# Memory attention on one core: tile 0's weights copied between tile 1's exponentials, tile 1's last transposes and values inside the first output product

## The reference, cut to what matters

```python
def memory_attention(h, mem_n, wq, wkv, wo):
    q = jnp.einsum('bsd,dhe->bshe', h, wq)
    kv = jnp.einsum('bmd,dche->bmche', mem_n, wkv)
    k, v = kv[:, :, 0], kv[:, :, 1]
    logits = jnp.einsum('bshe,bmhe->bhsm', q, k).astype(jnp.float32) * (X_DIM ** -0.5)
    p = jax.nn.softmax(logits, axis=-1)
    o = jnp.einsum('bhsm,bmhe->bshe', p.astype(v.dtype), v)
    return jnp.einsum('bshe,hed->bsd', o, wo)
```

## Time and profile before

| | us |
|---|---|
| median of 3 runs | 3042.37 (3041.61 to 3042.58) |
| the profiled execution's own time | 3040.55 |
| its span | 3038.8 |
| PE busy in the span | 3021.5 |
| ACT busy | 1536.7 |
| DVE busy | 1999.1 |

### The profile page before, as it was taken

The page is one execution under the profiler, slowest core; times in us unless marked ns, Lnnn a source line. Parts: engine busy times, 40 slices in busy tenths (PEclk is TensorE's granted clock), DMA queues, the critical chain, the costliest instruction groups (busy, mean ns, idle before and its releaser), DMA issues.

```text
span 3038.8 us, 43788 instructions
## 1 busy us (share of the span) xinstructions
PE 3021.5 (99%) x15684; PEld 2553.3 (84%) x15684; DVE 1999.1 (66%) x2366; ACT 1536.7 (51%) x2027; POOL 72.6 (2%) x122
## 2 busy tenths in 40 slices
PE   9999999999999999999999999999999999999999
PEld 9888888888888888888888888888888789788887
DVE  6677856555555555777857665655665778888664
ACT  6655546444444444655547455555554555444543
POOL 0000001000000000000000000000000010000000
PEclk9999999999999999999999999999999999999999
DMA  8764554655555555554554666666666555676555
GB/s 333 244 185 162 187 167 158 226 193 190 190 187 192 191 189 189 176 183 160 187 168 157 228 216 206 203 200 205 219 205 209 169 189 189 215 234 221 166 193 173
DMA packets 167930, 596.83 MB, mean 196 GB/s; under 512 B 18846, under 2 KB 26202, under 8 KB 164954
## 3 DMA queue, kind: packets, MB, share of 16 engines
q1 hardware_dynamic: 150432, 545.33, 54.4%
q10 hardware_dynamic: 14888, 36.86, 3.5%
q0 software_dynamic: 2464, 12.67, 1.3%
HBM read 577.99 MB, written 17.07 MB: 196 GB/s over the span
## 4 chain that ended last, share of the span: by engine, by line
PE 90%; DVE 6%; ACT 2%; DVEq 1%; issue 1%; DMA 0%; ACTq 0%; POOL 0%; POOLq 0%; SPq 0%
PE acc L741 24%; PE acc L743 23%; PE acc L742 23%; PE acc L747 3%; PE acc L756 3%; PE acc L759 3%; PE acc L758 3%; DVE lo L2006 2%; PE acc L749 2%; PE tp L831 1%; PE tp L873 1%; PE tp L1040 0%; PE tp L1273 0%; ACT hi L1331 0%; DVE sr L2806 0%
## 5 line engine op out<-in xcount | busy, mean ns | idle before, releaser
L2006 DVE TENSOR_TENSOR lo<-raw,hi 128x1024 fp32r<-128x1024 f32 x1032 | 1245.8, 1215 | 787.0 <-ACT hi L1331 775.8
L1331 ACT ACTIVATE hi<-raw 128x1024 fp32r<-128x1024 f32 x1032 | 1079.6, 1051 | 1133.4 <-PE acc L743 938.0
L741 PE MATMUL acc<-hi,xhl 128*128 128x512 f32 (+2 forms) x2472 | 958.7, 388 | 4.5 <-DVE xhl L2149 2.5
L743 PE MATMUL acc<-hi,xhl 128*128 128x512 f32 (+2 forms) x2472 | 951.2, 385 | 0.0
L742 PE MATMUL acc<-lo,xhl 128*128 128x512 f32 (+2 forms) x2472 | 950.6, 385 | 0.0
L741 PEld LDWEIGHTS acc<-hi,xhl 128*128 128x128 f32 x2472 | 464.3, 188 | 99.9 <-issue 8.1
L743 PEld LDWEIGHTS acc<-hi,xhl 128*128 128x128 f32 x2472 | 464.1, 188 | 92.5
L742 PEld LDWEIGHTS acc<-lo,xhl 128*128 128x128 f32 x2472 | 464.6, 188 | 88.7
L741 PE MATMUL acc<-hi,hTh 128*128 128x512 f32 x640 | 249.1, 389 | 0.0
L743 PE MATMUL acc<-hi,hTl 128*128 128x512 f32 x640 | 249.0, 389 | 0.0
L742 PE MATMUL acc<-lo,hTh 128*128 128x512 f32 x640 | 249.0, 389 | 0.0
(11 more groups left out here) (456 smaller groups left out, 2964.7 us busy)
## 6 DMA issues: line engine op xcount, KB each, us to landing
raw<-in_stream SPq DMA_DIRECT2D x1032, 512.0 KB, 4.2
turn_scratch<-made ACTq DMA_DIRECT2D x8, 1024.0 KB, 6.8
gpost<-in_post_g POOLq DMA_DIRECT2D x6, 1024.0 KB, 8.3
rotc<-turn_scratch ACTq DMA_DIRECT2D x8, 512.0 KB, 6.8
rots<-turn_scratch ACTq DMA_DIRECT2D x8, 512.0 KB, 8.6
u_stack<-u_scratch ACTq DMA_DIRECT2D x24, 128.0 KB, 4.8
h<-in_mem ACTq DMA_DIRECT2D x2, 1024.0 KB, 8.5
xT<-in_x_cols ACTq DMA_DIRECT2D x4, 512.0 KB, 6.7
```

The source lines that it names most:

```text
L741: nc.tensor.matmul(o, ah, high, start=first, stop=False)
L743: last = nc.tensor.matmul(o, al, high, start=False, stop=final)
L1331: nc.scalar.activation(hi[s][:, :, 0:w], raw[s][:, :, 0:w], ACT.Copy).then_inc(hi_done, 1)
L2006: nc.vector.tensor_tensor(lo[s][:, :, 0:w], raw[s][:, :, 0:w], hi[s][:, :, 0:w].bitcast(F32), ALU.subtract).then_inc(split_done, 1)
```

## The change

On ACT, tile 0's two copies (L1698 before) stand ahead of tile 1's second pair of exponentials, and tile 0's high half ahead of tile 1's copies. On PE, the values of tile 0 come straight behind the transposes of tile 0; the transposes (1,1) stand between the two units of `xo0`'s tile 0, and the values of tile 1 between tile 0 and tile 1 of `xo0`. The `stay_warm` matmuls are 4, 2, 2, 2 (10 in all) in place of 4, 3, 1, 1 (9), and the first four no longer wait for the PSUM buffer. DVE, POOL and SP have the same rows in the same order.

```diff
-                        tile_product(pos, LG["xo0"], a_h, a_l, lambda t: pe.wait_ge(x_split, pos.n(2, t + 1)))
+                        tile_product(pos, LG["xo0"], a_h, a_l, between)
...
                 for t in range(NT):
-                    tile_ready(t)
                     for n in range(g.units):
+                        tile_ready(t, n)
...
+                stay_warm(free.parity, xl[:, 8:10, :], 4)
+                weights_across(0, 0)
+                stay_warm(free.parity, xl[:, 8:10, :], 2)
+                weights_across(0, 1)
+                stay_warm(free.parity, xl[:, 8:10, :], 2)
+                head_values(0)
+                weights_across(1, 0)
+                stay_warm(free.parity, xl[:, 8:10, :], 2)
+
+                def second_tile_heads(t, n):
+                    if (t, n) == (0, 1):
+                        weights_across(1, 1)
+                    elif (t, n) == (1, 0):
+                        head_values(1)
+                    if n == 0:
+                        pe.wait_ge(x_split, pos.n(2, t + 1))
+
+                branch_products(pos, 1, "xo", cqh, cql, between=second_tile_heads)
...
+                head_exps(0, 0)
+                head_exps(0, 1)
+                head_exps(1, 0)
+                weights_copy(0, 0)
+                weights_copy(0, 1)
+                head_exps(1, 1)
+                values_high(0)
+                weights_copy(1, 0)
+                weights_copy(1, 1)
+                values_high(1)
```

More of the change, by code:

```diff
@@ L957, in given_rows, with branch_products @@
                 return unit_ready
-            def branch_products(pos, k, tag, a_h, a_l, quad_ready=None):
+            def branch_products(pos, k, tag, a_h, a_l, quad_ready=None, between=None):
                 for n in range(4):
@@ L1141, in _, with weights_across, head_values @@
                 values = acc[LG["xq"].parity]
[L1142 to L1154, removed]
+                def weights_across(i, m):
+                    o = take_turn(pe, pos, LTP[f"xT{i}"]) if m == 0 else tp[LTP[f"xT{i}"] % 2]
+                    pe.wait_ge(x_weights, pos.n(4, 2 * i + m + 1))
+                    for hd in (2 * m, 2 * m + 1):
+                        for b in range(NT):
+                            last = nc.tensor.transpose(o[:, hd, b * P:(b + 1) * P], xe[i][:, hd, b * P:(b + 1) * P],
+                                                       ident[:, :])
+                    last.then_inc((x_across, tp_full)[m], 1)
+                def head_values(i):
                     for m in range(2):
@@ L1161, in _ @@
                     last.then_inc(x_values, 1)
-                branch_products(pos, 1, "xo", cqh, cql)
+                stay_warm(free.parity, xl[:, 8:10, :], 4)
[14 more added lines that the diff above has]
+                branch_products(pos, 1, "xo", cqh, cql, between=second_tile_heads)
                 ready = raw_start(pos, 2, "fpre", LTP, LG["gate0"])
@@ L1680, in _ @@
                 nc.scalar.activation(small[:, 252:253], small[:, 253:254], ACT.Exp)
[L1681 to L1690, removed]
@@ L1691, in _ @@
-                for i in range(NT):
-                    o = tp[LTP[f"xT{i}"] % 2]
[L1693 to L1700, removed]
@@ L1701, in _, with head_exps @@
-                for i in range(NT):
+                def head_exps(i, m):
+                    act.wait_ge(x_max, pos.n(4, 2 * i + m + 1))
+                    o = tp[LTP[f"xL{i}"] % 2]
+                    for hd in (2 * m, 2 * m + 1):
+                        last = nc.scalar.activation(xe[i][:, hd, :], o[:, hd, :], ACT.Exp, scale=rsx[:, i:i + 1],
+                                                    bias=nmx[i][:, hd:hd + 1], accum_out=sm[i][:, hd:hd + 1])
+                    last.then_inc((x_exp, tp_read[LTP[f"xL{i}"] % 2])[m], 1)
@@ new lines, in weights_copy @@
+                def weights_copy(i, m):
+                    o = tp[LTP[f"xT{i}"] % 2]
+                    if m == 0:
+                        act.wait_ge(x_across, pos.n(2, i + 1))
+                    else:
+                        see_turn(act, pos, LTP[f"xT{i}"])
+                    nc.scalar.activation(xz[i][:, 2 * m:2 * m + 2, :], o[:, 2 * m:2 * m + 2, :], ACT.Copy)\
+                      .then_inc(x_copied, 1)
+                    if m == 1:
+                        act.drain().then_inc(tp_read[LTP[f"xT{i}"] % 2], 1)
@@ L1702, in _, with values_high @@
+                def values_high(i):
                     act.wait_ge(x_values, pos.n(2, i + 1))
```

## The result

The changed kernel takes 3045.98 us (median of 22 runs, 3044.53 to 3048.73); the kernel before, measured beside it, 3041.89 us (22 runs, 3039.55 to 3045.95). The ratio is 1.0015, with a 95% interval of 1.0009 to 1.0021: 2.7 to 6.4 us slower, and clear of no change. The forecast was 5.4 us slower, 3047.8, with a range of 3045.4 to 3050.0.

The account below looks back on a forecast made before the run. The prediction took PE to bound the kernel, busy 3021.5 of 3038.8 us. Its terms summed to 2.69 us later in each layer, 5.4 for two, so 3042.4 + 5.4 = 3047.8, range 3045.4 to 3050.0.

Parts of the forecast that it names:

- The chain of 3.37 us: Memory attention: from a tile's first value matmul through ACT and DVE to its product, 3.37 us, 1.62 of it ACT and DVE alone.
- The start of `xo0`: Product start in memory attention: 1.29 us sooner, at 16.72 against 18.01, once tile 0 is split.
- the front of the stage: First fillers and transposes (0,0): these start some 0.5 us sooner, without gain, since transposes (0,1) still wait for DVE.
- The exponentials "at no cost": ACT's exponentials (1,1) behind tile 0's copies: moved to about 13.75 to 14.95, costing nothing on the path, 0.15 us in hand.
- Two fillers more are on the path: PE's work before the products: two extra fillers at 0.23 us each counted as lengthening the path.
- the fourth rival: Whole kernel faster, at most 3041, if DVE finished sooner by some effect on shared PSUM traffic; chance 0.02.
- Tile 0 of `xo0` with the transposes (1,1): Inside the product: tile 0 takes 2.84 us as before, the transposes 0.49 more, so tile 1's values start at 20.05.
- The wait ahead of tile 1: PE before tile 1's product: 1.62 us idle, with nothing left to lie over ACT and DVE.
- The weight unit: ACT's split behind tile 1's high half: moves from 18.78 to 22.6, wanted at 29, cost nothing.
- The dearer joins: Three added fp32r/fp32 changes inside `xo0`: at 0.15 us a join, 3.1 a layer, 3048.6; chance 0.20.
- Later absorption: Behind the stage: part of the delay swallowed later, or the second wait shorter, 3044.3 to 3046; chance 0.12.
- The clock: Idle stretches in the stage: clock falls to half speed for 6 us, 3 us lost, twice, 3053.8; chance 0.06.

## Why the prediction was right, point by point

**The chain of 3.37 us** from a tile's first value matmul to its product. Measured for tile 1: values at 1623.95, product at 1627.31, 3.36 us. ACT's high half starts 1.98 behind the values, DVE's low half 0.63 behind that. This was the term that carried the forecast, and the run that put the values ahead of a unit of the product showed that it is the cause: the chain kept its 3.36 us there, and with a unit over it only 0.2 of the 1.6 us between PE's last slot and the product stayed bare.

**The start of `xo0`**, forecast at 10.94 (1616.72) and measured at 10.93 and 10.92. That it fits within 0.02 is in part luck, since three small errors cancel. "That gives nothing", of the front of the stage, was wrong: before, the transposes (0,1) start 0.19 us behind the end of DVE's product (12.28, then 12.47), not 0.06, so it was the third filler that set them. With one filler less they start 0.05 behind it, at 6.56 in place of 6.69 us, 0.13 sooner. From there to the values it is 0.95 us where 0.88 was forecast, so the values start at 7.51, 7.57 forecast. And from the values to `xo0` it is 3.41 and not 3.37.

**The exponentials "at no cost"**: right as a term of this change. But the cover was thinner than I wrote. I had only looked at PE's buffer and the transposes (1,1), and not at DVE, whose rows (1,1) stand ahead of the low half of tile 0: they end at 1619.88, the very time at which the low half starts. The two rows of DVE in the changed kernel:

```profile
1619.19 0.69 DVE L2553 TENSOR_TENSOR xe<-xe,small 128x512 f32<-128x512 f32 x1
1619.88 0.69 DVE L2567 TENSOR_TENSOR cql<-acc,cqh 128x512 fp32r<-128x512 f32 x1
```

One more delay on that path would have cost at once, and for that reason taking fillers out won next to nothing.

**"Two fillers more are on the path"**, in the check of the sum and in the fourth rival: wrong. Without the two behind the transposes (0,1) `xo0` starts 0.09 us sooner and not 0.45, and the two ahead of `xo0` stand in a wait. The sum did not suffer, since the path beside it has the same length; that tie was not foreseen, and that it did no harm is luck too.

**Tile 0 of `xo0` with the transposes (1,1)**: 20.05 - 16.72 = 3.33 forecast, 1623.95 - 1620.67 = 3.28 measured.

**The wait ahead of tile 1**: 1.62 forecast, 1.41 in the row. The same stretch is meant: mine began at the end of the last matmul's slot, the row begins when its result is out (3.36 - 1.75 = 1.61 and 3.36 - 1.95 = 1.41). Tile 1's own product takes 2.87, 2.84 forecast.

**The weight unit** that ACT splits behind the high half of tile 1: forecast at 22.6, measured at 1626.42 - 3.97 = 1622.45. It cost nothing, as forecast: behind the stage PE waits 0.5 us for such splits, 0.6 before.

**The dearer joins** (first rival): not so. From the transposes to the product's seventh matmul, 1622.13 to 1622.48, it is 0.35 us, and the seventh takes 0.32 to the next in place of 0.23: 0.44 together for what I had at 0.49. The rival asked for 0.15 at each join on top.

**Later absorption** (third rival): no sign. From the next product of the first layer to the logits of the second it is 1123.39 us before and 1123.37 after, and from the next product of the second layer to the end 1415.2 and 1415.4: nothing is given back. The runs give 4.1 us between the medians, with an interval that holds 5.3, and can't tell a swallowed 1 us from none. Why the medians lie 1.2 closer than the timelines say is open; the scatter would allow it.

**The clock** (second rival): 1.00 in both stages of the changed kernel. It falls in two of four stages when all fillers go, and then a fall costs 1.1 to 1.3 us, where I had put 3. Both of my rows for it were weak. The "half speed" of the transposes at the program's start is not in the granted clock, which the profile gives as 1.00 from 1.64 to 7.80 us; why they take 0.22 us each is not shown. And the program's end, where the clock held for some 3 us of idle time, did not show that shorter idle times are safe: without fillers it fell behind 1.22 and 1.02 us with four transposes between.

## What to carry to other kernels

A result that passes through two other engines before it can be used needs work of PE's own directly behind it, at least as long as their chain. Moving work "into" a product helps only if product matmuls are left between that work and the part that needs it: here one unit (1.4 us) between them, with four transposes (0.4 us) put into idle time, made the difference between 2.65 and 0.8 us lost in a layer. When a queue is reordered, follow each engine's program for what now stands behind the delayed instruction, even if its direct readers have time.

## What the runs showed of the hardware that was not expected

In the kernel without fillers, behind idle times of 1.22 and 1.02 us with only four transposes in between, the clock fell to half in two of four stages and stayed there for 3.4 us. The same place at full clock in the other two stages shows that these idle times alone do not decide it. With 1.41 us of bare waiting behind a row of 1.95 us of fp32 matmuls it fell in none of 12 stages: both layers of the changed kernel, of the ones of the exponentials' order, of two fillers less and of both, and of both profiles without fillers. Whether the transposes or the length of the sparse stretch made the difference was not tried.
